# Joint of two transformer blocks: last units by token tile, context and gates prepared among the down units, first retention head begun with its context half

## The reference

```python
# first block, one layer
mix = jnp.concatenate([o_a, o_b], -1) @ w_out
x = layer_norm(DEEPNORM_ALPHA * x + mix, ln1_g, ln1_b)
hid = causal_dwconv(x @ w_up, ffn_conv_w) + ffn_conv_b
gate, val = jnp.split(hid, 2, -1)
ffn = (jax.nn.silu(gate) * val) @ w_down
x = layer_norm(DEEPNORM_ALPHA * x + ffn, ln2_g, ln2_b)
# second block, layer 0 (retention, 4 heads, q and k of 256, v of 512)
h = x * (1.0 + sc1) + sh1          # sc, sh, g from silu(c) @ ada_w
hc = ctx * (1.0 + sc1c) + sh1c     # the same with c_ctx: no norm ahead
y, yc = retention_mixer(h, hc, ...)
x = layer_norm_2(DN_ALPHA * x + g1 * y, ln_g[i, 0], ln_b[i, 0])
```

## Time and profile before

| | |
|---|---|
| median of 3 runs | 2268.44 us (2266.93 to 2271.46) |
| the profiled execution | 2268.38 us, its span 2266.6 us |
| TensorE busy | 2079.5 us, 92% of the span |
| VectorE / ScalarE / POOL busy | 57% / 38% / 10% |
| last down unit of layer 1 | 941.77 to 947.37 us |
| first q product of the retention | 978.72 us |
| first v product of the retention | 1003.74 us |

### The profile page before, as it was taken

How to read it: one execution, slowest core, us unless ns; L and a number is a source line. 1 busy time by engine, 2 the same in 40 slices (tenths; PEclk the granted TensorE clock), 3 DMA queues, 4 the chain that set the end, 5 groups by cost and what they waited for, 6 DMA issues and landing times.

```text
span 2266.6 us, 31271 instructions
## 1 busy us (share of the span) xinstructions
PE 2079.5 (92%) x12171; PEld 1728.6 (76%) x12171; DVE 1300.8 (57%) x2064; ACT 865.3 (38%) x1435; POOL 220.3 (10%) x229
## 2 busy tenths in 40 slices
PE   5978899979889899879999999899999899897997
PEld 5856699869666798667777777788888688677896
DVE  4464677655645787544444447744434843766667
ACT  4433256434422465432232223432222332654443
POOL 2020200000010000000000000400000060532000
PEclk9999899989999899989999999899999899998999
DMA  7465756544576465522222222333332264425662
GB/s 212 131 232 177 209 149 175 190 117 149 175 233 204 136 181 186 167 68 75 74 74 74 86 75 63 93 93 93 93 93 93 93 122 130 57 48 146 183 191 93
DMA packets 304192, 296.32 MB, mean 131 GB/s; under 512 B 10406, under 2 KB 223602, under 8 KB 303968
## 3 DMA queue, kind: packets, MB, share of 16 engines
q1 hardware_dynamic: 297200, 276.86, 40.3%
q0 software_dynamic: 6896, 18.13, 3.7%
HBM read 293.90 MB, written 1.05 MB: 130 GB/s over the span
## 4 chain that ended last, share of the span: by engine, by line
PE 78%; DVE 14%; ACT 3%; issue 3%; DMA 1%; DVEq 0%; SPq 0%; ACTq 0%; POOL 0%; POOLq 0%
PE ps L424 21%; PE ps L426 21%; PE ps L425 21%; DVE w_lo L413 3%; PE ps L2203 2%; PE ps L1761 2%; PE ps L490 2%; DVE hid L1424 1%; PE ps L667 1%; PE ps L2193 1%; PE ps L665 1%; PE ps L2216 1%; PE ps L1744 1%; DVE npr L2309 1%; PE ps L657 1%
## 5 line engine op out<-in xcount | busy, mean ns | idle before, releaser
L413 DVE TENSOR_TENSOR w_lo<-raw,w_hi 128x1024 fp32r<-128x1024 f32 x428 | 524.6, 1267 | 410.2 <-ACT w_hi L405 410.0
L405 ACT ACTIVATE w_hi<-raw 128x1024 fp32r<-128x1024 f32 x428 | 428.9, 1051 | 618.7 <-PE ps L424 508.1
L424 PE MATMUL ps<-zt_hi,w_hi 128*128 128x512 f32 (+1 forms) x784 | 273.0, 348 | 18.2 <-DVE zt_lo L2465 7.9
L424 PE MATMUL ps<-xt_hi,w_hi 128*128 128x256 f32 x896 | 258.9, 289 | 23.8 <-DVE xt_lo L1102 10.0
L425 PE MATMUL ps<-zt_lo,w_hi 128*128 128x512 f32 (+1 forms) x784 | 271.8, 347 | 0.0
L426 PE MATMUL ps<-zt_hi,w_lo 128*128 128x512 f32 (+1 forms) x784 | 271.5, 346 | 0.0
L425 PE MATMUL ps<-xt_lo,w_hi 128*128 128x256 f32 x896 | 255.0, 285 | 0.0
L426 PE MATMUL ps<-xt_hi,w_lo 128*128 128x256 f32 x896 | 254.8, 284 | 0.0
L424 PEld LDWEIGHTS ps<-xt_hi,w_hi 128*128 128x128 f32 x896 | 172.9, 193 | 29.9 <-issue 12.2
L424 PEld LDWEIGHTS ps<-zt_hi,w_hi 128*128 128x128 f32 x784 | 150.0, 191 | 39.5 <-issue 11.6
L425 PEld LDWEIGHTS ps<-xt_lo,w_hi 128*128 128x128 f32 x896 | 173.1, 193 | 0.0
(11 more groups left out here) (369 smaller groups left out, 3559.3 us busy)
## 6 DMA issues: line engine op xcount, KB each, us to landing
raw<-in_mlp_w SPq DMA_DIRECT2D x128, 512.0 KB, 4.6
raw<-in_ada_w SPq DMA_DIRECT2D x96, 512.0 KB, 4.9
raw<-in_w_up SPq DMA_DIRECT2D x88, 512.0 KB, 5.0
raw<-in_w_in SPq DMA_DIRECT2D x56, 512.0 KB, 4.7
raw<-in_ret_w_in SPq DMA_DIRECT2D x48, 512.0 KB, 4.4
raw<-in_w_down SPq DMA_DIRECT2D x44, 512.0 KB, 4.1
raw<-in_nat_w_in SPq DMA_DIRECT2D x24, 512.0 KB, 5.1
raw<-in_w_out SPq DMA_DIRECT2D x16, 512.0 KB, 5.3
```

The lines of the kernel that those rows point to most:

```text
L405: nc.scalar.activation(w_hi[:, t, w], raw[:, s, w], ACT.Copy).then_inc(on("w_hi"), act.gives("w_hi"))
L413: ins = nc.vector.tensor_tensor(w_lo[:, t, w], raw[:, s, w], w_hi[:, t, w].bitcast(F32), ALU.subtract)
L424: first = nc.tensor.matmul(out_ap, l_hi, r_hi, start=start, stop=False)
```

## The change

It has six parts.

1. The last w_out unit of each layer runs tile by tile (`rows_by_tile`) and signals `y_ps` per tile.
2. So does the last down unit of each layer; `dve_norm` waits per tile.
3. In the second layer, the gates are broadcast behind the third down unit, and TensorE waits for their copies behind the fifth.
4. The context is loaded a second time into `xc0`, transposed behind the fifth down unit, and modulated by ScalarE between its splits (n = 5 and 7). VectorE makes its low part behind the latents' statistics (`behind_sums`), before their norm.
5. The first head has its q and k products written out (`pe_first_qk`), 256 columns at a time: the context's with the latents' transposes between them, then the latents'. The loop over heads keeps two turns.
6. `gate_b` moves to another place; the last head waits for `xc_in`. VectorE makes the low part of the second retention unit ahead of the latents' low parts.

```diff
@@ pe_mixer
                 for c in range(2):
+                    if j == 0 and c == 1:
+                        rows_by_tile(pe, [ps[6 + t][:, :] for t in range(NT)], xt_hi, xt_lo, range(4), False, True,
+                                     sem="y_ps")
+                        continue
@@ pe_ffn
-            for j in range(FT // 2):
+            for j in range(FT // 2 - 1):
                 pe.eng.wait_ge(on("h"), pe.takes("h", 2))
                 rows_product(pe, [[ps[t][:, :], ps[2 + t][:, :]] for t in range(NT)], h_hi, h_lo,
-                             (2 * j, 2 * j + 1), j == 0, j == FT // 2 - 1,
-                             "y_ps" if j == FT // 2 - 1 else None, n_k=2, width=D)
-            pe.eng.wait_ge(on("conv_f"), pe.takes("conv_f", 2))
+                             (2 * j, 2 * j + 1), j == 0, False, None, n_k=2, width=D)
+                if j == 2:
+                    pe.eng.wait_ge(on("conv_f"), pe.takes("conv_f", 2))
+                    if l + 1 == DEPTH:
+                        pe.eng.wait_ge(on("coef"), pe.takes("coef"))
+                        pe_gates(pe, 0, 2, (0, 1))
+                if j == 4 and l + 1 == DEPTH:
+                    pe_gates_end(pe, (0, 1))
+                    pe.eng.wait_ge(on("xc0_in"), pe.takes("xc0_in", 16))
+                    for t in range(NT):
+                        pe_turned(pe, xc0[:, t, :], (4 + 2 * t, 5 + 2 * t))
+            pe.eng.wait_ge(on("h"), pe.takes("h", 2))
+            hi, lo = unit_slot(pe)
+            for t in range(NT):
+                x = slice(t * P, (t + 1) * P)
+                for j in range(2):
+                    for c in range(2):
+                        w = slice(j * D + c * 512, j * D + (c + 1) * 512)
+                        first, last = three(ps[2 * c + t][:, :], h_hi[:, FT - 2 + j, x], h_lo[:, FT - 2 + j, x],
+                                            hi[:, w], lo[:, w], False, j == 1)
+                        if t == j == c == 0:
+                            begun(pe, first)
+                last.then_inc(on("y_ps"), pe.gives("y_ps"))
+            if l + 1 == DEPTH:
+                pe.eng.wait_ge(on("c_hi"), pe.takes("c_hi", NT))
             release(pe)
@@ act_ffn
-            for _ in range(FT // 2):
+            for n in range(FT // 2):
                 split_hi(act)
+                if l + 1 == DEPTH:
+                    if n == 3:
+                        act.eng.wait_ge(on("coef"), act.takes("coef"))
+                        act_gates(act, (0, 1))
+                    if n in (5, 7):
+                        act_context(act, (n - 5) // 2)
@@ dve_norm
-            dve.eng.wait_ge(on("y_ps"), dve.takes("y_ps"))
             if halves == 2:
+                dve.eng.wait_ge(on("y_ps"), dve.takes("y_ps"))
                 for t in range(NT):
                     residual(0, t)
+            for t in range(NT):
                 dve.eng.wait_ge(on("y_ps"), dve.takes("y_ps"))
-            for t in range(NT):
                 for c in range(halves - 1, 2):
                     residual(c, t)
                 dve.eng.wait_ge(on("v_step"), dve.given("v_step"))
                 dve_statistics(dve, xs[:, t, :], t)
+            if behind_sums:
+                behind_sums()
...
+            if fine is not None:
+                split_lo(dve)
@@ pe_ret
+        def pe_first_qk(pe):
+            hi, lo = {}, {}
+            def product(n, stream, f):
+                x = slice(stream * SEQ, (stream + 1) * SEQ)
+                for k in range(KT):
+                    c = f * 1024 + k * P
+                    first, last = three(ps[2 * n + f][:, x], hi[n][:, c:c + P], lo[n][:, c:c + P], zt_hi[:, k, x],
+                                        zt_lo[:, k, x], k == 0, k == KT - 1)
+                    if k == 0 and f == 0 and stream == n:
+                        begun(pe, first)
+                return last
+            def turned(t):
+                pe.eng.wait_ge(on("xn"), pe.takes("xn"))
+                pe_turned(pe, xs[:, t, :], (4 + 2 * t, 5 + 2 * t))
+            hi[0], lo[0] = unit_slot(pe)
+            pe.eng.wait_ge(on("xT"), pe.takes("xT", NT))
+            product(0, 0, 0)
+            turned(0)
+            product(0, 0, 1)
+            turned(1)
+            hi[1], lo[1] = unit_slot(pe)
+            product(1, 0, 0)
+            product(1, 0, 1)
+            pe.eng.wait_ge(on("xT"), pe.takes("xT", NT))
+            for n in range(2):
+                product(n, 1, 0)
+                product(n, 1, 1).then_inc(on("proj_ps"), pe.gives("proj_ps"))
@@ gpsimd
                 pool_norm(pool)
-                pool.eng.wait_ge(on("y_ps"), pool.takes("y_ps", 3))
+                if l + 1 == DEPTH:
+                    eng.dma_start(xc0[:, :, :], a["ctx_2"].rearrange("b (t p) d -> p (b t) d", p=P)).then_inc(
+                        on("xc0_in"), pool.gives("xc0_in", 16))
+                pool.eng.wait_ge(on("y_ps"), pool.takes("y_ps", 5))
```

More of the change, by code:

```diff
@@ L282, in build @@
         hid = sbb("hid", [4, 2, SEQ])
+        xc0 = sbb("xc0", [NT, D])
         pb.close()
@@ L294, in build @@
         xc = s2("xc", [NT, D])
-        gate_b = s2("gate_b", [2, D])
         pc = ExitStack()
@@ L321, in build @@
         hh_lo = sm("hh_lo", [2, 4, 2 * SEQ], F32R)
+        gate_b = sm("gate_b", [2, D])
         pm2.close()
@@ L757, in pe_norm, with pe_ffn @@
             pe.eng.wait_ge(on("xT"), pe.takes("xT", NT))
-        def pe_ffn(pe):
+        def pe_ffn(pe, l):
             def up(j):
@@ L1061, in act_norm, with act_context, act_ffn @@
                         on("x_hi"), act.gives("x_hi"))
-        def act_ffn(act):
+        def act_context(act, t):
+            act.eng.wait_ge(on("xnt_ps"), act.takes("xnt_ps"))
+            for k in range(KT):
+                A.activation(xf1[:, t, k, :], ps[4 + 2 * t + k // 4][:, hs(k % 4)], ACT.Identity,
+                             scale=coef[:, 0, 0, k:k + 1], bias=coef[:, 0, 1, k:k + 1]).then_inc(
+                                 on("a_step"), act.gives("a_step"))
+            act.eng.wait_ge(on("a_step"), act.given("a_step"))
+            act_copy(zt_hi[:, :, t * P:(t + 1) * P], xf1[:, t, :, :]).then_inc(on("c_hi"), act.gives("c_hi"))
+        def act_ffn(act, l):
             def up(j, f):
@@ L1375, in dve_statistics, with dve_norm @@
                 on("pow_in"), dve.gives("pow_in"))
-        def dve_norm(dve, halves, n, hi, lo, fine=None):
+        def dve_norm(dve, halves, n, hi, lo, fine=None, behind_sums=None):
             bank = 4 - 4 * n
@@ L1412, in dve_norm @@
                 ins.then_inc(on("xT"), dve.gives("xT"))
-            split_lo(dve)
+            if fine is None:
+                split_lo(dve)
         def dve_ffn(dve):
@@ L1730, in pe_ret, with pe_head @@
         def pe_ret(pe):
[L1731 to L1735, removed]
-            for n in range(2):
-                up_unit(pe, [ps[2 * n][:, :], ps[2 * n + 1][:, :]], zt_hi, zt_lo, "proj_ps")
+            pe_head(pe, first_head=True)
+            with pe.turns("ret", RH - 2):
+                pe_head(pe)
+            pe_head(pe, last_head=True)
+        def pe_first_qk(pe):
+            hi, lo = {}, {}
+            def product(n, stream, f):
+                x = slice(stream * SEQ, (stream + 1) * SEQ)
+                for k in range(KT):
+                    c = f * 1024 + k * P
[17 more added lines that the diff above has]
+            pe.eng.wait_ge(on("xT"), pe.takes("xT", NT))
+            for n in range(2):
+                product(n, 1, 0)
+                product(n, 1, 1).then_inc(on("proj_ps"), pe.gives("proj_ps"))
+        def pe_head(pe, first_head=False, last_head=False):
+            if first_head:
+                pe_first_qk(pe)
+            else:
+                for n in range(2):
+                    up_unit(pe, [ps[2 * n][:, :], ps[2 * n + 1][:, :]], zt_hi, zt_lo, "proj_ps")
             for j in range(2):
@@ L1898, in dve_head @@
                 dve.eng.wait_ge(on("y_add"), dve.given("y_add"))
+                dve.eng.wait_ge(on("xc_in"), dve.takes("xc_in", 16))
                 dve.eng.wait_ge(on("gate_b"), dve.takes("gate_b", 4))
@@ L2423, in _ @@
                 act_norm(act, xt_hi, 0)
-                act_ffn(act)
+                act_ffn(act, l)
                 if l + 1 < DEPTH:
                     act_norm(act, xt_hi)
-            act.eng.wait_ge(on("coef"), act.takes("coef"))
-            act_gates(act, (0, 1))
+            act.eng.wait_ge(on("xT"), act.takes("xT", (2 * DEPTH - 1) * NT + NT))
             act_norm(act, zt_hi[:, :, SEQ:2 * SEQ], mods=(coef[:, 1, 0, :], coef[:, 1, 1, :], xf1))
[L2431 to L2439, removed]
             act_ret(act)
@@ L2460, in _, with context @@
                     dve_norm(dve, 1, 1, xt_hi, xt_lo)
[L2461 to L2466, removed]
+            def context():
+                for t in range(NT):
+                    dve.eng.wait_ge(on("c_hi"), dve.takes("c_hi"))
+                    x = (slice(None), slice(None), slice(t * P, (t + 1) * P))
```

(6 more changed lines are left out.)

## The result

The changed kernel took 2249.81 us (median of 5, 2245.9 to 2259.1) beside 2268.44 for the kernel before: a ratio of 0.991, 95% interval 0.989 to 0.993. Two more comparisons on other chips gave 0.9923 (0.9907 to 0.9939) and 0.9889 (0.9871 to 0.9907). The 17 times of the three, each divided by the mean of before on its chip, have a mean of 0.9907: a gain of 21.1 us, give or take 2.9 at 95% with the spread of before's means counted in. The forecast was 2248.9, a gain of 19.55.

What follows compares the result with a forecast made beforehand. TensorE was taken as the bound, its work off counting only where it waits, chiefly at the joint of the two blocks. 2268.4 - 16.4 (joint) - 3.15 (smaller terms) = 2248.9 us; own range 2245.5 to 2251, wider 2243 to 2255.5.

Steps and rivals of the forecast that it cites:

- T+5.7: New end of the last down unit against the old end T: gates 3.8 us plus context transposes 1.9, all paid.
- Rival 3: Down units: ScalarE's context work and gate copies push splits beyond the cover, 2.8 us; 2251.7 to 2255.5 us; chance 0.06.
- VectorE's order: Behind the last down unit: both tiles' sums, then context subtractions, then norm; TensorE may start at T'+6.9.
- T': The end of the last down unit in the changed kernel, from which the joint's forecast times count.
- The first 24 products: First group of the first head's narrow q and k products, at the low clock: 0.21 us each, 5.1 us.
- The prediction's bounds: Low clock at the joint's start lasts 3.4 to 5.8 us, 5.3 counted: -0.9 to +0.3 us of time added.
- rival 2: Low clock comes twice, again when TensorE waits for a normed tile or the latents; 2251.5 us; chance 0.09.
- Latents ready at T'+22.25: First head: ScalarE starts tile 0 at T'+13.2, 9.05 us to the last low part; within 0.2 us of TensorE's products.
- The third weight unit: Behind rope table, decay and clearing of y, its low part comes late: TensorE waits 0.5 us, begins at T'+34.3.
- Rival 1: First head's preparation bounds: rope load and clearing come later, 2 to 5 us wait; 2251 to 2255 us; chance 0.13.
- Narrow products: First head's 192 q and k products of 256 columns: 0.117 us each, 22.4 us in sum, same as 96 wide.
- Smaller terms: By-tile order: 1.85 us at layer 0's last down unit, 0.65 at each of two last w_out units; 3.15 together.

## Why the prediction was right

**Down units: T+5.7, measured +5.39.** Gates and context transposes ran at the high clock without a wait. They were priced at 0.12 us each, but the 3.82 us of the earlier trace rows count the last product to its end; from start to next start the 32 took 3.49 us and the 16 took 1.66. From TensorE's and ScalarE's timelines of after:

```profile
912.23 0.60 PE L1548 MATMUL ps<-cst,xc 128*128 128x128 f32 x4
```

```profile
907.12 2.01 ACT L406 ACTIVATE w_hi<-raw 128x1024 fp32r<-128x1024 f32 x2 [3.60 <-PE ps L425]
909.04 2.03 ACT L935 ACTIVATE gate_b<-ps 128x512 f32<-128x512 f32 x4
...
920.07 2.01 ACT L406 ACTIVATE w_hi<-raw 128x1024 fp32r<-128x1024 f32 x2 [3.58 <-PE ps L425]
921.98 2.87 ACT L1093 ACTIVATE xf<-ps,coef 128x128 f32<-128x128 f32 x8
924.89 1.06 ACT L935 ACTIVATE zt_hi<-xf 128x1024 fp32r<-128x1024 f32 x1
925.86 1.99 ACT L406 ACTIVATE w_hi<-raw 128x1024 fp32r<-128x1024 f32 x2
```

The four gate copies lie in one idle time of ScalarE; a context tile pushes the next split back with no idle time left, and TensorE doesn't notice. Doubled, the same work cost 5.6 us. Rival 3 is out, and by a measured cover rather than by luck.

**VectorE's order.** Forecast: tile 0 from T'-1.65, sums done at T'+4.25, context low parts at T'+6.7, TensorE at T'+6.9. Measured with T' = 947.57: -1.73, +4.16 (951.73, where the context begins), +6.51, +6.66.

**The first 24 products: too dear by 0.8.** 5.1 us forecast, 4.32 measured (954.23 to 958.55). The price came from the execution of before, where the clock stayed low for 5.8 us; it doesn't always. In the six profiles with this start the 24 products took 4.27 to 5.26 us. The granted clock over the first and the next 3 us behind the start, in after, in its third profile, and in the kernel with ScalarE's work doubled:

```profile
954.23:957.23 3.00, 3.00 (x14) 3.00 (x15) 2.96 (x3) 0.00 (x0) 0.00 (x0) 0.50 0.00 0
957.23:960.23 3.00, 3.00 (x27) 3.00 (x27) 2.96 (x4) 0.55 (x2) 0.00 (x0) 0.98 0.00 0
```

```profile
956.05:959.05 3.00, 3.00 (x14) 3.00 (x15) 2.96 (x3) 0.00 (x0) 0.00 (x0) 0.50 0.00 0
959.05:962.05 3.00, 3.00 (x22) 3.00 (x22) 2.96 (x4) 0.00 (x0) 0.00 (x0) 0.74 0.00 0
```

```profile
963.22:966.22 3.00, 3.00 (x14) 3.00 (x15) 2.96 (x3) 0.00 (x0) 0.00 (x0) 0.50 0.00 0
966.22:969.22 3.00, 3.00 (x17) 3.00 (x17) 2.96 (x4) 0.00 (x0) 0.00 (x0) 0.55 0.00 0
```

Always 0.50 at first, then 0.98, 0.74, 0.55: the same wait of 6.5 us leaves a low stretch of some 3 to 5.7 us. The prediction's bounds nearly had this (3.4 and 5.8); it took 5.3, near the upper one, and after fell just below the lower. In the kernel with ScalarE's work doubled the forecast would have met it: 5.26 us, and the latents at T'+22.3. So the mechanism was right, and the execution decides which end of the range comes. It was low once, not twice, so rival 2 is out for the change (it came true, in small, with the context made ahead).

**Latents ready at T'+22.25, measured +21.18** (968.75). TensorE then began on them 0.2 us later than its own products would have let it, so this path came last of the two, where the forecast had it 0.15 us ahead. The whole difference is there when ScalarE starts on tile 0: 959.68, that is T'+12.1 against 13.2. From ScalarE's start to the last low part 9.07 us passed (9.05 forecast).

**The third weight unit: a wait of 0.5, measured 0.9.** Forecast: clearing done 9.46 us behind the latents, low part 2.36, v product at T'+34.3. Measured: 9.88 (978.63), 2.29, and 980.89 = T'+33.32. ScalarE's and VectorE's timelines of after, against the earlier trace rows:

```profile
968.04 1.28 ACT L1873 ACT_TABLE_LOAD   x1
973.80 0.21 ACT L1873 ACTIVATE rsm<-rsm 128x8 f32<-128x8 f32 x1 [4.47 <-DMA rsm<-in_ret_decay]
```

```profile
977.72 0.91 DVE L1914 MEMSET y<- 128x1024 f32 x1 [0.16 <-issue]
978.54 2.29 DVE L414 TENSOR_TENSOR w_lo<-raw,w_hi 128x1024 fp32r<-128x1024 f32 x2
```

It is the chain that the forecast named, and moving the clearing takes it away. It was 0.4 us longer than forecast (9.8 to 10.2 in the four profiles that have it), since the exponential began 5.0 to 5.3 us behind the latents and not 4.6. Rival 1 had the right place and too high a price: the wait was 0.9, 1.2 and 0.5 us in the three profiles of the change and 1.2 in the doubled one, not 2 to 5.

**Narrow products: 0.117 forecast, 0.113 to 0.118 measured.** The timeline of after has both, and the experiment without overlap shows that nothing else hid a cost. Here the row beat the rule: "TensorE: Matmul & The Clock Gate" of the Trainium skill (Back-to-back issue gap) would have the weight load count in the spacing; with a load to each product the spacing was half of the 0.233 us of 512 columns.

**Smaller terms: 3.15 forecast, 3.33 measured** (1.84, 0.75, 0.74). None was given back by a later wait.

What was off: 0.3 us too much in the down units and 1 us too much behind them, the low clock above all. The gain of 21.0 by stretches and of 21.1 by the three comparisons lies 1.5 us above the forecast's 19.55, well inside its range. Two prices of the rivals don't follow from their terms: a wait of 5 us in place of 0.5 gives rival 1 at most 2253.4, not 2255, and 2253.3 with the 3.15 of by-tile gains lost gives rival 3 2256.5, not 2255.5. Neither bears on the forecast.

## What to carry to other kernels

Behind a long idle time of TensorE, look first for work whose inputs are ready earlier, and give it the start of the next stage, even if its products become narrower: where the pitch goes by columns at half the width (find such a row in the trace before), splitting is free, as the 24.45 us here show, and the other half's preparation disappears under it. Small TensorE work moved into a stage that TensorE bounds was paid in full here (5.4 us), and ScalarE's work beside it was free up to the slack in one unit and paid in full beyond: count the slack per unit, not the mean busy share. Here the next path lay within a microsecond once the idle time was filled, so list what stood behind it in each engine's order before pricing a further step. And read a step worth 3 us from its stretch: the whole time hid it.

## What the runs showed of the hardware

- The low clock behind the same idle time of 6.5 us lasted from some 3 us (0.50, then 0.98) to 5.7 us (0.50, then 0.55) over six profiles of the same start. The 24 products there took 4.27 to 5.26 us, and 4.27 to 4.96 over three executions of one and the same kernel.
- An idle time of 3.1 us left the clock high for the next eight transposes (1.07 us), where 5.0 us had not (1.94): a shorter wait can win more than its own length. This is one profile against two, and the eight transposes after the next 1.35 us of idle time ran at the low clock.
- 192 products of 256 columns, each with a load of its own, took 24.45 us, and 96 of 512 took 25.02, the low-clock start in both. At the high clock the starts of the narrow ones were 0.113 to 0.118 us apart.
- Stretches whose code was the same in all kernels differed by 1.8 us (up units) and 5.4 us (layer 1's mixing) from one profiled execution to another, more than most of the terms argued over here. In the mixing part of it is the granted clock, 0.72 in place of 1.00 over the same 6 us.
